# Moving two modulation groups behind attention and three row gathers into the expert stage

## What is computed

```python
# first block
mix = token_mixer(x, w_in, sinks, w_proj_a, w_proj_b, w_out, slopes)   # two kinds of attention, gated, merged
x = layer_norm(DEEPNORM_ALPHA * x + mix, ln1_g, ln1_b)
ffn = moe_ffn(x, router_w, ...)                  # 32 experts, top 4 of them for each token
x = layer_norm(DEEPNORM_ALPHA * x + ffn, ln2_g, ln2_b)

# second block: two layers, on the latent x and on a context of 256 rows
sc, sc_ctx = jax.nn.silu(c), jax.nn.silu(c_ctx)
for i in range(2):
    m = (sc @ w_mod[i] + b_mod[i]).reshape(bsz, 6, d)       # shifts, scales and gates of layer i
    mc = (sc_ctx @ w_mod[i] + b_mod[i]).reshape(6, d)       # the same for the context
    ...                                                     # mixer: chunk MLP (i = 0), linear attention (i = 1)
    x = layer_norm_2(DN_ALPHA * x + g1 * mix_lat, ln_g[i, 0], ln_b[i, 0])
    ffn_lat = peer_ffn(x * (1.0 + s2) + sh2, p_w_q[i], p_keys[i], p_u[i], p_v[i])
    ...                                                     # the context too, while i = 0

# peer_ffn: 8 heads, 16 of 16384 small experts each, whose rows are gathered by index
act = jax.nn.gelu(jnp.einsum('thkd,td->thk', u_tab[idx], xb)) * wts
out = jnp.einsum('thk,thkd->td', act, v_tab[idx])
```

## Time and profile before

| | |
|---|---|
| three runs | 3639.62, 3647.6, 3646.48 us; median 3646.48 |
| the profiled execution | 3643.52 us, span 3641.7 us |
| PE (TensorE) busy | 3219.5 us, 88% |
| DVE (VectorE) busy | 1761.2 us, 48% |
| ACT (ScalarE) busy | 1088.3 us, 30% |
| POOL (GpSimd) busy | 862.0 us, 24% |
| HBM read | 1376.48 MB, 378 GB/s over the span |
| mean granted TensorE clock | 0.97 of 2.4 GHz |

### The profile page before, as it was taken

One profiled execution on the slowest core, in us unless ns is written; L12 is line 12 of the kernel. 1 busy time (PEld: TensorE's weight loads), 2 busy tenths in 40 slices (PEclk: granted clock), 3 DMA queues, 4 the chain that ended last, 5 costly groups with the idle time before them and its releaser, 6 DMA issues. The chain is left out here.

```text
span 3641.7 us, 34378 instructions
## 1 busy us (share of the span) xinstructions
PE 3219.5 (88%) x11268; PEld 1436.6 (39%) x11268; DVE 1761.2 (48%) x4096; ACT 1088.3 (30%) x2958; POOL 862.0 (24%) x796
## 2 busy tenths in 40 slices
PE   8898899999999996988888878998888978788776
PEld 6476443344334432433344323333334444222222
DVE  0053211111130124776775677668764466766665
ACT  1131111111111112344343344445334123433433
POOL 0100000000000002443444444444441014444432
PEclk9999899999999998999999999999999989999999
DMA  9934799999999999999999999999997149999997
GB/s 406 427 118 152 289 408 416 422 417 425 412 428 428 399 428 374 408 421 422 421 417 409 420 420 415 407 417 415 419 413 303 49 191 421 421 421 420 417 411 328
DMA packets 158245, 1379.94 MB, mean 379 GB/s; under 512 B 18601, under 2 KB 19113, under 8 KB 26610
## 3 DMA queue, kind: packets, MB, share of 16 engines
q0 software_dynamic: 111360, 805.46, 53.5%
q1 hardware_dynamic: 46706, 572.24, 37.7%
HBM read 1376.48 MB, written 1.15 MB: 378 GB/s over the span
## 5 line engine op out<-in xcount | busy, mean ns | idle before, releaser
L2701 PE MATMUL ps<-sb_arena,sb_diag 128*128 128x512 f32 x3072 | 1498.4, 626 | 337.3 <-ACT sb_diag L2678 335.4
L2604 POOL DMA_INDIRECT sb_arena<-in_uv,sb_idx x768 | 849.3, 1106 | 2586.2 <-POOLq L1278 1229.0
L2637 DVE SCALAR_TENSOR_TENSOR sb_arena<-sb_arena,sb_H 128x1024 f32<-128x1024 f32 x768 | 940.8, 1226 | 623.5 <-DMA sb_arena<-in_uv,sb_idx 418.6
L2701 PEld LDWEIGHTS ps<-sb_arena,sb_diag 128*128 128x128 f32 x3072 | 565.3, 196 | 1226.4 <-ACT sb_diag L2678 657.1
L1357 PE MATMUL ps<-sb_ring,sb_arena 128*64 128x512 f32 x3072 | 674.3, 594 | 3.6 <-DMA sb_ring<-in_moe 3.6
L2669 ACT ACTIVATE sb_act<-sb_dots 128x1 f32<-128x1 f32 x768 | 155.0, 202 | 1102.7 <-DVE sb_arena L2637 1100.9
L1357 PEld LDWEIGHTS ps<-sb_ring,sb_arena 128*64 128x64 f32 x3072 | 214.4, 137 | 441.5 <-issue 430.5
L2678 ACT ACTIVATE sb_diag<-sb_consts,sb_act 128x128 f32<-128x128 f32 x768 | 308.4, 402 | 26.7 <-PE ps L2701 1.6
L1547 DVE TENSOR_SCALAR sb_arena<-ps 128x512 f32<-128x512 f32 x32 | 22.1, 692 | 591.4 <-PE ps L1357 575.7
L2673 ACT ACTIVATE sb_act<-sb_act,sb_wts 128x1 f32<-128x1 f32 x768 | 226.2, 295 | 24.9
L179 PE MATMUL ps<-sb_ring,sb_arena 128*128 128x512 f32 x416 | 182.0, 594 | 1.9 <-DVE sb_arena L700 1.3
(11 more groups left out here) (347 smaller groups left out, 2374.6 us busy)
## 6 DMA issues: line engine op xcount, KB each, us to landing
sb_ring<-in_moe SPq DMA_DIRECT2D x192, 2048.0 KB, 16.3
sb_ring<-in_w_mod SPq DMA_DIRECT2D x24, 2048.0 KB, 20.3
sb_ring<-in_w_in SPq DMA_DIRECT2D x10, 2048.0 KB, 25.6
sb_ring<-in_a_w_in SPq DMA_DIRECT2D x8, 2048.0 KB, 13.4
sb_ring<-in_b_w_in SPq DMA_DIRECT2D x8, 2048.0 KB, 11.9
sb_ring<-in_w_q SPq DMA_DIRECT2D x6, 2048.0 KB, 11.4
sb_arena<-in_uv,sb_idx POOLq DMA_INDIRECT x768, 15.2
sb_ring<-in_a_w_out SPq DMA_DIRECT2D x4, 2048.0 KB, 16.3
```

The source lines that it names most:

```text
L2604: pool.indirect_dma_start(uv[n_ % BUFS], None, table, bass.IndirectOffsetOnAxis(m.idx[:, pair % 2, k:k + 1], 0))\
L2637: nc.vector.scalar_tensor_tensor(out=u, in0=u, scalar=1.0, in1=m.H[:, order[i], :], op0=ALU.mult, op1=ALU.mult, accum_out=m.dots[:, n_ % P ...
L2701: last = nc.tensor.matmul(out[h], m.diag[n_ % DIAGS], uv[b][:, D + h * 512:D + (h + 1) * 512], start=opens, stop=ends)
```

## The change

1. The last two of the six modulation groups (numbers 4 and 5, `LATE_MODS = 2`) leave the first stage. Their eight chunks stand behind `w_out` in the ring. Group 4 is computed in `attention` after the out products, group 5 in `route` between the logits and the wait for `gates_known`. ScalarE and GpSimd follow with their copies and stores at the end of their lists in the same blocks.
2. SP sends the two norm rows ahead of `w_mod17`, and the first chunk of expert 0 in `route` instead of `attention`.
3. The first three gathers of layer 0 (`EARLY = 3`) are issued at the end of `moe`, once the first indices are known and the last expert chunk has landed. They need buffers that are free there, so the eight buffers are used in another order.

The core of the diff:

```diff
+LATE_MODS = 2
...
+class Modulation:
...
+    def tensor(self, pe, i):
+        nc, m, M, banks, ring, where = self.nc, self.m, self.M, self.banks, self.ring, self.where[i]
+        banks.wait_free(pe, where)
...
+    def store(self, pool, i):
+        pool.wait_ge(self.M("mod_staged"), i + 1)
+        for g in range(4):
+            col = (4 * (i % (N_MOD // 2)) + g) * 512
+            pool.dma_start(self.d["mod"][i // (N_MOD // 2), :, col:col + 512], self.stage[32 * g:32 * g + 2, i % 2, :])\
+                .then_inc(self.M(f"mod_out{i % 2}"), 16)
...
+    early = N_MOD - LATE_MODS
+    mod.plan(range(early), [6, 7])
...
         @block.gpsimd
         def _(pool):
-            for i in range(n_mod):
...
+            for i in range(early):
+                mod.store(pool, i)
             for i in range(2):
-                pool.wait_ge(M(f"mod_out{i}"), 64 * (n_mod // 2))
+                pool.wait_ge(M(f"mod_out{i}"), 64 * (early // 2))
+            mod.store(pool, early)
...
-            ring.load(sp, ring.at["moe0.0"] + 4)
+            ring.load(sp, ring.at["w_out"] + 3)

             sp.wait_ge(M("merged_ready"), KT)
             load_rows(sp, M, m, [d["lns"][i:i + 1, :] for i in range(2)], norm_rows)
-            ring.load(sp, ring.at["moe0.0"] + PER_EXPERT)
+            ring.load(sp, ring.at["moe0.0"])
...
-                    modulation(n // 2 - 1)
+                    if n // 2 <= early:
+                        mod.tensor(pe, n // 2 - 1)
...
-                    modulation(4 + piece)
+                    if 4 + piece < early:
+                        mod.tensor(pe, 4 + piece)
...
                     ring.done(pe, "w_out", half)
+            mod.tensor(pe, early)
...
             for t in range(TT):
                 norm_act(nc, act, m, M, n0 + t + 1)
+            mod.scalar(act, early)
...
+    mod.plan([N_MOD - 1], [7])
     with nc.Block() as block:
+
+        @block.gpsimd
+        def _(pool):
+            mod.store(pool, N_MOD - 1)
+            for i in range(2):
+                pool.wait_ge(M(f"mod_out{i}"), 64 * (N_MOD // 2))
...
+            mod.tensor(pe, N_MOD - 1)
             pe.wait_ge(M("gates_known"), TT)
...
+            mod.scalar(act, N_MOD - 1)
...
+        @block.gpsimd
+        def _(pool):
+            pool.wait_ge(M("idx_ready"), 1)
+            end = ring.at[f"moe{NE - 1}.{PER_EXPERT - 1}"]
+            pool.wait_ge(M(f"chunk_in{ring.chunks[end][3]}"), 16 * (ring.nth[end] + 1))
+            for n in range(EARLY):
+                gather_rows(nc, pool, d, m, M, 0, n, 0, n)
...
+BUFFER_ORDER = (0, 6, 7, 1, 2, 3, 4, 5)
+EARLY = 3
...
-                pool.indirect_dma_start(uv[n_ % BUFS], None, table, bass.IndirectOffsetOnAxis(m.idx[:, pair % 2, k:k + 1], 0))\
-                    .then_inc(M(f"uv_in{n_ % BUFS}"), 16)
+                if n_ >= EARLY:
+                    gather_rows(nc, pool, d, m, M, layer, n_, pair, k)
...
-            if 1 <= n <= N_MOD:
+            if 1 <= n <= N_MOD - LATE_MODS:
                 front += [(f"w_mod{u}", d["w_mod"][u], SLOT) for u in range(4 * n - 4, 4 * n)]
...
         front += [("w_out", d["w_out"][n], SLOT) for n in range(2)]
+        front += [(f"w_mod{u}", d["w_mod"][u], SLOT) for u in range(4 * (N_MOD - LATE_MODS), 4 * N_MOD)]
```

More of the change, by code:

```diff
@@ L269, in attention @@
+def attention(nc, d, m, M, banks, ring, mod):
     qk = m.part(0, 21, T)
@@ L296, in attention @@
     gp = banks.plan(proj, [0, 1, 2, 3])
-    c = rows[:, 3592:3608].rearrange("p (k s) -> p k s", k=KT)
-    silu_c = rows[:, 3608:3624].rearrange("p (k s) -> p k s", k=KT)
-    bias = m.part(15872, 512)
-    stage = m.part(12800, 2, 512)
-    n_mod = N_MOD
-    mods = banks.plan([("mod", i) for i in range(n_mod)], [6, 7])
+    early = N_MOD - LATE_MODS
+    mod.plan(range(early), [6, 7])
     go = banks.plan([("o", u) for u in range(len(units))], [6])
@@ L312, in attention @@
     gx = banks.plan([("x", i) for i in range(4)], [4, 5, 6, 7])
+    mod.plan([early], [0])
     with nc.Block() as block:
```

116 lines of the change are left out of this document (61 added, 55 removed).

## The result

The changed kernel takes 3654.95 us (median of 8 runs, 3652.38 to 3657.6) against 3642.41 for the kernel before (8 runs beside it, 3639.16 to 3649.32): 12.5 us more, a ratio of 1.0030 with a 95% interval of 1.0019 to 1.0041. The forecast was +4.4 to 3650.9 us, "same", with a range of 3636 to 3661. The time lies in that range. In time the forecast missed by 4.0 us, in difference by 8.1: the kernel before was at 3642.41 in its eight runs and not at the 3646.48 of the three from which the prediction started, and that part of the closeness is luck. The profiled executions are 3655.8 and 3641.7 us of span, 14.1 apart.

What follows compares the result with a forecast made beforehand. The kernel was taken as a DMA-bound stream of weights and gathered rows with two holes. Profiled 3643.5 - 18.4 + 6.5 + 21.3 - 5.0 = 3647.9 (+4.4), on the median 3650.9 us; range 3636 to 3661.

Steps and rivals of the forecast that it cites:

- same: Whole kernel: a difference within 0.2% (7.3 us) either way, about what a measurement can tell from none; chance 0.52.
- First stage, -18.4: Start to first scores: without groups 4 and 5, w_in6 follows w_in5 directly on TensorE; 18.4 us saved.
- Attention's end, +6.5: After the out products: group 4's products, copies and stores all on the path, ending at 368.2 against 361.6; +6.5 us.
- Routing, +21.3: Routing block: slowed TensorE clock, group 5 and late chunk loads delay the expert stage's opening; +21.3 us.
- The chain of group 5's slots, four chunks and the context rows: Routing's end: expert chunks 2 to 5 wait for group 5's slots, then context rows; expert stage opens at 413.1.
- Expert stage, 0: Expert stage: same six chunks in the ring, TensorE cold as now, same loads; change of 0.
- Early gathers, -5.0: End of the expert stage: gathers fill the DMA hole behind the last expert chunk; 5 us saved, ends 0 and 7.5.
- Rival 1: Gathers' opening: VectorE sets the pace, early gathers buy nothing; +9.4, 3655.9 us; chance 0.28 with all that overshoots.
- the third gather only displaces what follows: Expert stage's end: two gathers of 2.5 us fit the DMA hole, a third gains nothing more.
- slower: Whole kernel: more than 7.3 us slower than before; chance 0.28.
- second condition: Sign for slower: the two stages before the gathers cost 2.9 us more than summed, as with a late router load.
- Rival 2: Routing swallows the late work, so most of +21.3 goes: 3629.6 us wholly hidden, 3640 half hidden; chance 0.17.

Runs made afterwards that it cites:

- stores_moved: The change, with group 4's four stores issued at the start of routing instead of attention's end: 3652.40 us against 3644.31 for the kernel before, 1.0022.
- ctx_first: The change, with the context rows issued ahead of routing's expert chunks instead of behind the last: 3651.89 us against 3643.73 for the kernel before, 1.0021.
- one_late_ctx: one_late, with the context rows issued ahead of the expert chunks: 3648.27 us against 3645.71 for the kernel before, 1.0008.
- gathers_only: The change without late groups: all six groups stay early, three early gathers and the buffers' order kept: 3637.06 us against 3644.31 for the kernel before, 0.9980.
- one_late_free: one_late, with context rows ahead of the expert chunks and group 5's stores issued in the expert block: 3633.98 us against 3643.73 for the kernel before, 0.9974.
- both_free: The change, with both late groups' stores issued in the expert block and context rows ahead of the chunks: 3632.63 us against 3645.71 for the kernel before, 0.9966.
- one_late: The change with only group 5 late, in routing, and group 4 back in the first stage: 3653.36 us against 3643.73 for the kernel before, 1.0027.
- warm: The change plus 36 extra TensorE matmuls of constants behind routing's placement products, result unread: 3663.26 us against 3644.31 for the kernel before, 1.0056.

## Why the prediction was right and wrong

*First stage, -18.4: right* (-17.6 at the scores, -19.1 at the out products). The point that eight chunks of DMA are not 39.3 us of time, because TensorE paces that stretch, holds.

*Attention's end, +6.5: the step that failed.* The prediction ended it with "four stores 2.04 plus 0.3 of release", and +13.0 was measured. The issue of a store is not its end: 6.7 us passed from the last issue (349.28) to the next block's first load (356.02), where the sum had 0.3. Everything ahead of it in this term was right: the copies were to end at 347.3 and ended at 346.6. The price was in reach: the 24 stores of the kernel before took 6.6 us to land in the median, and the prediction itself gave group 5's stores "a few us to land", and then hid them under the chunks; at attention's end there is nothing to hide them, since every engine waits there. stores_moved adds the second half of the answer: without this wait the router's weights would have held the logits, and only 2.3 of the 8.7 us would be gained. A term for attention's end has to name both. (The prediction did see the weights queue behind w_mod22 and w_mod23, for 1.5 us; in the change they cost 0.78 us of wait, as the 0.84 before, since the stores' landing covered the rest.)

*Routing, +21.3: right in size (+20.4) and in mechanism.* The chain of group 5's slots, four chunks and the context rows held the opening; ctx_first and one_late_ctx removed it and gained 5.4 and 7.0 us at the opening. It was not alone: the stores' landing ended 5 to 7 us ahead of it, and held the block once the chain was gone. The clock fell between group 4 and routing as said; it rose inside group 5, whose chunk products took 9.20 us, against 7.05 for group 4's at full clock. The measured +20.4 rests on one execution of each kernel, and routing took 22.96 us in the one of before and 21.0 in gathers_only, so a difference of a microsecond or two from the forecast would have meant little.

*Expert stage, 0 ("TensorE cold as now"): right as an expectation, wrong as a certainty.* In the traces the opening takes 17.1 to 24.3 us to the first load, mostly by when the clock rises, and 19.0 and 24.3 in two executions of one and the same code. The profiled execution of before was near the short end and that of after at the long end. The term needed a range of some 5 us, and the prediction gave it none.

*Early gathers, -5.0: right* (4.1 over eleven traces, 5.8 in the one pair). Rival 1 falls on its own ground: VectorE had its first dot 1.9 us behind the first late gather, and at the fourth it waited for data, not the data for it. The working by which the third gather only displaces what follows is not confirmed.

*The rivals.* By the median slower came true in the prediction's own terms (more than 7.3 us; the interval, about 7 to 15, just reaches that), though not by rival 1's mechanism. Its second condition, that "the two stages before cost 2.9 us more than summed", is what happened: 13.0 + 20.4 - 19.1 = +14.3 at the opening against +9.4 summed. Rival 2 falls for the change (nothing was swallowed; the opening came 14.3 later), yet its mechanism is in part what one_late_free and both_free build. With neither the stores nor the chain at the block's end, group 5 hides in part under VectorE's selection: in one_late_free the placement products start 11.9 us behind the logits, in before 6.8, so that the group costs 5.1 us there.

Put together: 4.4 + 6.5 (the stores' landing) - 0.7 (first stage) - 0.9 (routing) + 0.9 (gathers) = +10.2, against 12.5 measured with an interval of about 7 to 15. The 2.3 between them are assigned to nothing; the opening's clock could hold them.

## What to carry to other kernels

In this kernel a step moved to the end of a block cost its last store's landing, not its issue; try stores whose reader is far off in the next block. When a move makes one wait, list every other thing that would end shortly behind it, because removing the first wait only uncovers the second: here 8.7 us became 2.3, while two edits together shortened the way from the placement products to the expert stage by 17 (one_late to one_late_free). And where a stage opens with the clock low, give its opening a range; one profiled execution is one draw.

## What the hardware showed beyond that

- Small stores from GpSimd take long to be acknowledged: four stores of 4 KB, 5.5 to 7.1 us from issue to landing (medians by kernel and place), 6.4 to 8.0 from the end of the last issue to the next work, both with DMA full (one_late_free) and with it running dry (the change, 350 to 355, DMA share 0.54). Eight of them in both_free took 7.5 and 10.1. The Trainium skill, "DMA: Bandwidth & Descriptors", Anatomy of one DMA (SWDGE path), gives a fit of 2.0 us plus the bytes over 436 GB/s, which would be, as an estimate, 2.0 us for 4 KB. No run here shows so little, and the measurement decides.
- The clock can fall with TensorE busy all the time: in warm, from 1.00 to 0.50 within 3 us of the opening, under 32-row bias products, after 31 us without a gap above 0.30 us.
- One stage of one program took 19.0 us from its opening to its first load in one execution and 24.3 in another, by the moment at which the clock rose (in 392 to 394 us and in 404 to 406).
